# Reordering the seven-product groups of the two down projections in a macaron transformer layer on one Trainium2 core

## The reference

```python
def swiglu(x, w_gate, w_up, w_down):
    return (jax.nn.silu(x @ w_gate) * (x @ w_up)) @ w_down
...
    f = swiglu(rmsnorm(h, g_ffn1_pre[i]), w_ffn1_gate[i], w_ffn1_up[i], w_ffn1_down[i])
    h = h + 0.5 * rmsnorm(f, g_ffn1_post[i])
```

## Time and profile before

| | us |
|---|---|
| runs (3): median, lowest, highest | 1903.43, 1902.51, 1903.64 |
| profiled execution, its own time | 1907.09 |
| its span | 1905.3 |
| TensorE (PE) busy in it | 1868.6 (98%) |
| VectorE (DVE) busy | 1253.8 (66%) |
| ScalarE (ACT) busy | 938.5 (49%) |
| DMA, mean | 195 GB/s |

### The profile page before, as it was taken

How to read it: one execution, slowest core, us unless ns; L and a number is a source line. 1 busy time by engine, 2 the same in 40 slices (tenths; PEclk the granted TensorE clock), 3 DMA queues, 4 the chain that set the end, 5 groups by cost and what they waited for, 6 DMA issues and landing times.

```text
span 1905.3 us, 24370 instructions
## 1 busy us (share of the span) xinstructions
PE 1868.6 (98%) x8562; PEld 1528.3 (80%) x8562; DVE 1253.8 (66%) x1400; ACT 938.5 (49%) x1239; POOL 112.9 (6%) x162
## 2 busy tenths in 40 slices
PE   9999999999999999999999999999999999999998
PEld 7888888888777778888888888888888887777886
DVE  5555554555797778787896755555554579867775
ACT  6444443444455446555565644444443455445563
POOL 1000000000000000012651100000000000000010
PEclk9999999999999999999999999999999999999999
DMA  8666666666555555655556566666666655655654
GB/s 258 206 201 206 194 191 204 217 214 211 198 191 198 159 185 183 201 168 165 157 180 200 165 212 207 203 205 201 200 192 198 221 200 185 209 187 183 213 189 144
DMA packets 214116, 371.55 MB, mean 195 GB/s; under 512 B 16592, under 2 KB 41632, under 8 KB 213664
## 3 DMA queue, kind: packets, MB, share of 16 engines
q1 hardware_dynamic: 213040, 367.20, 61.1%
q10 hardware_dynamic: 1008, 3.46, 0.5%
HBM read 358.01 MB, written 2.10 MB: 189 GB/s over the span
## 4 chain that ended last, share of the span: by engine, by line
PE 81%; DVE 12%; DMA 5%; ACT 1%; SPq 0%; issue 0%; DVEq 0%; POOLq 0%; POOL 0%; ACTq 0%
PE bank L654 26%; PE bank L656 25%; PE bank L655 25%; DVE w_rest L1539 7%; DMA raw<-in_w_ffn_down 5%; DVE branch L1551 1%; DVE branch L1547 1%; DVE branch L1549 1%; DVE branch L1546 1%; ACT w_high L1154 1%; PE bank L993 1%; PE bank L1022 1%; PE bank L1004 1%; PE bank L760 1%; DMA resid<-in_x 0%; PE bank L968 0%
## 5 line engine op out<-in xcount | busy, mean ns | idle before, releaser
L1525 DVE TENSOR_TENSOR w_rest<-raw,w_high 128x1024 fp32r<-128x1024 f32 x486 | 596.8, 1231 | 467.3 <-ACT w_high L1136 464.3
L1136 ACT CAST w_high<-raw 128x1024 fp32r<-128x1024 f32 x486 | 509.6, 1051 | 637.0 <-PE bank L656 493.2
L654 PE MATMUL bank<-w_high,x_high 128*128 128x512 f32 (+1 forms) x1912 | 745.7, 390 | 0.7 <-DVE x_rest L1966 0.2
L656 PE MATMUL bank<-w_high,x_rest 128*128 128x512 f32 (+1 forms) x1912 | 741.0, 388 | 0.0
L655 PE MATMUL bank<-w_rest,x_high 128*128 128x512 f32 (+1 forms) x1912 | 740.6, 387 | 0.0
L654 PEld LDWEIGHTS bank<-w_high,x_high 128*128 128x128 f32 x1912 | 359.1, 188 | 74.6 <-issue 1.6
L656 PEld LDWEIGHTS bank<-w_high,x_rest 128*128 128x128 f32 x1912 | 359.0, 188 | 73.8
L655 PEld LDWEIGHTS bank<-w_rest,x_high 128*128 128x128 f32 x1912 | 359.2, 188 | 71.6
L1539 DVE TENSOR_TENSOR w_rest<-raw,w_high 128x1024 fp32r<-128x1024 f32 x136 | 164.6, 1222 | 78.8 <-ACT w_high L1154 78.4
L1154 ACT CAST w_high<-raw 128x1024 fp32r<-128x1024 f32 x136 | 140.5, 1049 | 114.1 <-DMA raw<-in_w_ffn_down 58.3
L654 PE MATMUL bank<-w_high,h_high 128*128 128x512 f32 x448 | 176.3, 394 | 7.5 <-DVE w_rest L1539 7.5
(11 more groups left out here) (209 smaller groups left out, 1277.0 us busy)
## 6 DMA issues: line engine op xcount, KB each, us to landing
raw<-in_w_ffn_up SPq DMA_DIRECT2D x176, 512.0 KB, 4.6
raw<-in_w_ffn_gate SPq DMA_DIRECT2D x174, 512.0 KB, 4.4
raw<-in_w_ffn_down SPq DMA_DIRECT2D x144, 512.0 KB, 4.8
raw<-in_w_qkv SPq DMA_DIRECT2D x68, 512.0 KB, 4.0
branch<-in_w_ffn_down SPq DMA_DIRECT2D x32, 512.0 KB, 6.7
raw<-in_w_o SPq DMA_DIRECT2D x32, 512.0 KB, 4.2
raw<-in_w_ple_gate SPq DMA_DIRECT2D x32, 512.0 KB, 4.2
branch<-branch SPq DMA_DIRECT2D x320, 32.0 KB, 1.9
```

Of the source, the lines that this page charges most:

```text
L654: nc.tensor.matmul(o[:, 0:width], xh, wh, start=first and c == 0, stop=False, skip_group_check=go_on)
L656: ins = nc.tensor.matmul(o[:, 0:width], xr, wh, start=False, stop=last and c == chunks - 1, skip_group_check=go_on)
L1136: nc.scalar.copy(slot(n, k)[0], raw[:, k]).then_inc(w_high_done, 1)
L1525: nc.vector.tensor_tensor(to_rest, raw[:, k], to_high.bitcast(F32), ALU.subtract).then_inc(w_rest_done, 1)
```

## The change

The table is rewritten: a group's seven products alternate with four plain slots that stand inside it, in the order plain, `b11`, plain, `sum1`, `b22`, plain, `sum3`, `sum2`, `b21`, plain, `sum4`, and groups stand one behind another. Each sum is made right behind the rest of the block that completes it: sum1 behind `b11`, sum3 and sum2 behind `b22`, sum4 behind `b21`. The two in-place buffers change roles from group to group (`FIRST_OF`, `SECOND_OF`), so that the next `b11` goes where `sum3` has been read and the next `b12` where `sum4` has; the first group of j = 0 uses `gain_row` for one of them. The chain loads stand at places of their own in SyncE's queue (`CHAIN_AT`), the first one ahead of the stage; the gain loads follow later. Numbers of matmuls, casts, rests, sums and loads stay as they are.

```diff
     def group(i, inner):
 
-        return ([(kind, None, i) for kind in ("b22", "b21", "b11", "sum1", "sum3", "sum2")] + inner
-                + [("sum4", None, i)])
+        own = [(kind, None, i) for kind in ("b11", "sum1", "b22", "sum3", "sum2", "b21", "sum4")]
+        return inner[0:1] + own[0:1] + inner[1:2] + own[1:3] + inner[2:3] + own[3:6] + inner[3:4] + own[6:]
...
+    PAIR_ORDER = (plains(0, G0, G0 + 5) + group(0, plains(0, G0 + 5, G0 + 9)) + group(1, plains(1, G0, G0 + 4))
+                  + group(2, plains(0, G0 + 9, G0 + 11) + plains(1, G0 + 4, G0 + 6))
+                  + group(3, plains(1, G0 + 6, G0 + 10)) + plains(0, G0 + 11, FS) + plains(1, G0 + 10, FS))
...
-    COMBINE_AT = [0] + [at - 7 for at in GROUP_AT[1:]]
+    def after_op(t):
+
+        return min(u for r, u in enumerate(RING_OPS) if r >= RING and RING_OPS[r - RING] >= t)
+
+    CHAIN_AT = [[RING_OPS[RING]] * 2] + [[after_op(PLACE[end, None, i - 1]) for end in ("sum3", "sum4")] for i in range(1, GROUPS)]
+    FIRST_OF = [["row", 1, 0, 1], [0, 1, 0, 1]]
+    SECOND_OF = [[1, 0, 1, 0], [1, 0, 1, 0]]
+    COMBINE_AT = [0] + [at - 5 for at in GROUP_AT[1:]]
...
+    ODD_STOP = G0 + 9
...
+                def chain_load(j, i, b):
+
+                    if i == 0 and j == 0:
+                        if b:
+                            sp.wait_ge(turned, u_h + BPB)
+                    elif i == 0:
+                        sp.wait_ge(fixed_even, 2 * f + 1)
+                    elif i == 1 and j == 0 and b == 1:
+                        sp.wait_ge(turned, u_h + BPB)
+                    else:
+                        end = "sum4" if b else "sum3"
+                        sp.wait_ge(w_rest_done, n0 + PAIR_OPS * j + PLACE[end, None, i - 1] + 1)
+                    to = chain(j, (SECOND_OF if b else FIRST_OF)[j][i])
+                    sp.dma_start(to, part(2 * i, 2 * j + b)).then_inc(chain_landed[b], 16)
+
+                chain_load(0, 0, 0)
...
+                        for g in range(GROUPS):
+                            for b in range(2):
+                                if t == CHAIN_AT[g][b] and (j, g, b) != (0, 0, 0):
+                                    chain_load(j, g, b)
...
-                            pe.wait_ge(branch_ready, CREDIT - 1 + 2 * NBD * f + 2 * j + 1)
-                            pe.wait_ge(turn_rest, u_h + BPB)
+                            pe.wait_ge(turn_rest, u_h + BPB)
+                        if kind == "b22" and i == 0:
+                            pe.wait_ge(branch_ready, CREDIT - 1 + 2 * NBD * f + 2 * j + 1)
...
-                        if j == 0 and t - 1 in COMBINE_AT:
+                        if j == 0 and t - 2 in COMBINE_AT:
...
+                if kind in ("b11", "b22", "b21"):
+                    turns, other = chain(j, FIRST_OF[j][i]), chain(j, SECOND_OF[j][i])
+                    if kind == "b11":
+                        dve.wait_ge(chain_landed[1], 16 * (groups + i + 1))
+                        nc.vector.tensor_tensor(turns, turns, other, ALU.add).then_inc(sum_ready, 1)
+                    elif kind == "b22":
+                        nc.vector.tensor_tensor(other, other, src, ALU.add).then_inc(sum_ready, 1)
+                        nc.vector.tensor_tensor(turns, turns, src, ALU.add).then_inc(sum_ready, 1)
+                    else:
+                        nc.vector.tensor_tensor(turns, turns, src, ALU.add).then_inc(sum_ready, 1)
...
-                    dve.wait_ge(w_used, n0 + PAIR_OPS * j + PLACE["sum2", None, GROUPS - 1] + 1)
+                    dve.wait_ge(w_used, n0 + PAIR_OPS * j + PLACE["plain", 1, ODD_STOP] + 1)
```

More of the change, by code:

```diff
@@ L479, in down @@
                             sp.dma_start(raw[:, k], src).then_inc(w_landed[k], 16)
-                        if kind == "b22":
-                            for b, end in ((0, "sum4"), (1, "sum3")):
-                                if i:
-                                    sp.wait_ge(w_rest_done, n0 + PAIR_OPS * j + PLACE[end, None, i - 1] + 1)
-                                elif j:
-                                    sp.wait_ge(fixed_even, 2 * f + 1)
-                                else:
-                                    sp.wait_ge(turned, u_h + BPB)
-                                sp.dma_start(chain(j, b), part(2 * i, 2 * j + b)).then_inc(chain_landed[b], 16)
+                        if j == 0 and t == CHAIN_AT[1][1]:
+                            gain_load(0)
+                            gain_load(1)
                         if j and t == GROUP_END[0]:
@@ L1148, in high_down @@
                     act.wait_ge(chain_landed[0], 16 * (groups + i + 1))
-                    src = chain(j, 0)
+                    src = chain(j, FIRST_OF[j][i])
                 else:
                     act.wait_ge(sum_ready, 4 * (groups + i) + SUM_AT[kind])
-                    src = chain(j, 1 if kind == "sum3" else 0)
+                    src = chain(j, (SECOND_OF if kind == "sum3" else FIRST_OF)[j][i])
                 act.wait_ge(w_used, n - RING + 1)
@@ L1532, in rest_down @@
                 groups = GROUPS * (2 * f + j)
-                turns, b12 = chain(j, 0), chain(j, 1)
                 if kind in RING_KINDS:
@@ L1536, in rest_down @@
                 else:
-                    src = b12 if kind == "sum3" else turns
+                    src = chain(j, (SECOND_OF if kind == "sum3" else FIRST_OF)[j][i])
                 dve.wait_ge(w_high_done, n + 1)
@@ L1540, in rest_down @@
                                         ).then_inc(w_rest_done, 1)
-                if kind == "plain" or kind in ("b22", "b21", "sum3", "sum4"):
-                    return
-                b22, b21 = (raw[:, ring_item(j, PLACE[name, None, i])[1]] for name in ("b22", "b21"))
-                if kind == "b11":
-                    dve.wait_ge(chain_landed[1], 16 * (groups + i + 1))
-                    nc.vector.tensor_tensor(turns, turns, b12, ALU.add).then_inc(sum_ready, 1)
-                    nc.vector.tensor_tensor(b12, b12, b22, ALU.add).then_inc(sum_ready, 1)
-                elif kind == "sum1":
-                    nc.vector.tensor_tensor(turns, turns, b22, ALU.add).then_inc(sum_ready, 1)
-                else:
-                    nc.vector.tensor_tensor(turns, turns, b21, ALU.add).then_inc(sum_ready, 1)
+                if kind in ("b11", "b22", "b21"):
[6 more added lines that the diff above has]
+                        nc.vector.tensor_tensor(turns, turns, src, ALU.add).then_inc(sum_ready, 1)
+                    else:
+                        nc.vector.tensor_tensor(turns, turns, src, ALU.add).then_inc(sum_ready, 1)
             def ahead(n, s0, count_, k0=0):
```

33 lines of the change are left out of this document (16 added, 17 removed).

## The result

The changed kernel takes 1884.55 us (median of 4 runs, 1883.42 to 1885.65), the kernel before on the same chip 1902.97 (4 runs, 1902.31 to 1903.64): a ratio of 0.9903, 95% interval 0.9886 to 0.992, 18.4 us less. The forecast was 1875.4 with a range of 1866 to 1889; the result lies in the range, and outside the 1871 to 1882 that had the chance of 0.62. The profiled execution took 1885.05 us, its span 1883.3.

The account below looks back on a forecast made before the run. TensorE, busy 98% of the span, waits in the down stages only for VectorE's rests. Of 39.0 us possible, 5.7 (`combine`) and 4.7 (start) stay, leaving 28.6, taken as 28: median 1903.4 to 1875.4, range 1866 to 1889.

Parts of the forecast that it names:

- What there was to win: Both down stages: 41.1 us too long together, of which up to 39 us can be won.
- Combine, 5.7 us: Later groups of j = 0: third plain slot's rest 0.8 us late plus 0.15 restart, six times; 5.7 us stay.
- In j = 0 `combine` covers it: Groups of j = 0: VectorE's wait for the `b12` load is hidden by `combine`; cost zero.
- The start, 4.7 us: Start of each stage: loads queued behind the one waiting for `turned` make rests late, 2.35 us a stage; 4.7 stay.
- Fifth: just in time: Stage start: fifth slot's load lands at 498.3, its rest ends at 500.7, PE wants it at 500.9.
- j = 1 at zero: Groups of j = 1: VectorE's walk has nothing late, tightest rest 0.8 us to spare; zero stall.
- rival (b): `b12` late everywhere, taking 6.7 us and landing at 2.5: 16.5 us more, 1892; chance 0.15, or part of it.
- (c): Slower: `b12` takes the burst's 9.0 us, lands at 4.8, and the queue's head-of-line wait takes over: 1918; chance 0.04.
- The tail at zero: Stage end: four plain slots (10.9 us) cover even fix, squares and output, some 7 us; cost zero.
- the gain comes from order alone: Down stages: PE's matmuls, casts, rests, sums and bytes stay, so only their reordering brings the gain.
- (a): All stalls go, late j = 0 slots and start absorbed: 1864.4, or 1868 with one term halved; chance 0.14.
- (d): No change: the stall only moves, since VectorE's work is the same; 1903; chance 0.03.

Follow-up runs that it names:

- the second profile: The kernel before, unedited, profiled once more: 1903.39 us, span 1901.6.
- the later chain load: Changed kernel with the chain load that waits for `turned` put two ring loads later in SyncE's queue: 1877.41 us, ratio 0.9866.
- sum1 later: Changed kernel with sum1 made behind P1's rest (the group's second plain slot) instead of in front of it: 1884.4 us, ratio 0.9901.
- the one with slots between: The 1877.41 us kernel (first chain load two ring loads later) with a plain slot put ahead of the second and third group: 1873.67 us.
- the kernel with the shorter tail: The 1873.67 us kernel's two slots between groups, both taken from behind the last group, leaving one even slot there: 1887.17 us.
- the kernel with the seven together: Changed kernel with a group's seven products standing nearly together again, loads, buffers, roles and sum places kept: 1896.77 us, ratio 0.997.
- the kernel with three slots: The 1873.67 us kernel with a third plain slot, ahead of the fourth group, and `fix_odd` one operation earlier: 1874.37 us.

## Why the prediction was right, and where it wasn't

**Right: the sign, what PE waits for, and the place of most of what stays.** PE waits for rests 12 times, where "about 6 + 6, all in j = 0, each under 1.2 us" stood: 11 are in j = 0, and the longest is 1.30. Two of the forecast's own signs of error came: a wait for the fifth slot, and one wait in j = 1. The change won 18.4 us where 28 were forecast, so nearly all terms were too hopeful. The forecast's sum was 39.0 possible less 5.7 less 4.7, taken as 28. Against the profile that it was made from, 22.7 us went from the stages. Its terms:

- *What there was to win* was too large by about 4 us, since it was read from one profiled execution: its first stage was 4.0 us longer than in the second profile. The forecast moved its result by 3.7 us to the median, but took the gain whole, though the excess lay just where the gain was counted. This is the largest single error, 3 to 4 of the 9 us by which the forecast missed.
- *Combine, 5.7 us* ("0.8 us late, and 0.15 for the restart" in each of six groups): measured 7.1 by the gaps, 7.3 by leaving it out. The walk was right in its chain, and in its size too where VectorE doesn't stand for b12: gaps of 1.05 to 1.12 us (three with the later chain load, five with sum1 later) are 0.9 to 1.0 with the restart, and it has 0.95. What it missed is b12. "In j = 0 `combine` covers it" failed in four of six groups, by 0.18 to 0.48 us and 1.3 in all, so in the second group the third slot's rest began at 9.4 on its clock instead of 9.1. Nothing is handed on from group to group, although VectorE's work in such a group, 15 starts of 1.135, one `combine` of 2.86 and one `combine_rest`, is 21.0 us against 20.4 of TensorE: in all six the rest of the first plain slot begins 4.1 us ahead of its product, as the walk has it. A plain slot ahead of the group lets it begin 5.5 us ahead, and that is what removes the gap. The second group's `combine`, which follows that rest by 1.14, and the product, in the changed kernel and in the one with slots between:

```profile
525.38 1.22 DVE L1746 TENSOR_TENSOR branch<-h_high,h_rest 128x1024 f32<-128x1024 f32 x1
...
528.35 0.39 PE L679 MATMUL bank<-w_high,h_high 128*128 128x512 f32 x1
```
```profile
520.15 1.22 DVE L1747 TENSOR_TENSOR branch<-h_high,h_rest 128x1024 f32<-128x1024 f32 x1
...
524.47 0.39 PE L680 MATMUL bank<-w_high,h_high 128*128 128x512 f32 x1
```

- *The start, 4.7 us*: gaps and restarts sum to 3.4 in the first stage and 2.1 in the second, 5.5. "Fifth: just in time" failed in the first stage, where PE stood 1.30 us for it (gap 1.69 at 503.14): its load took 6.5 us from issue, landing at 500.66, and not 498.3, in a row of five that followed 1.3 apart. The cause was named, the queue behind `turned`. The later chain load gives back 7.1 us by the medians: these 5.5, and 0.7 in the combined groups, where VectorE stands less for b12. The rest lies in j = 1 of the first stage and isn't the start's, as said above.
- *j = 1 at zero*: about 1.5 us, beside 0.8 for the transposes at the first stage's end and the 1.0 of the undisturbed half. The only waits, at 671.50 (gap 0.88) and behind, follow a b12 load of 6.5 us, over the "5.6" that the text gave as the limit; those of 5.2 to 5.6 left no gap. This is rival (b), once in six groups. One ring load later, b12 takes 6.1 us, goes out 1.8 later, and the time goes to 1908: the thin cover was thin, and (b) and (c) are one slope. They price 16.5 us more for a landing at 2.5 on the group's clock and 43.5 more at 4.8 (49 less the 5.7 of `combine`); b12 lands at 3.1 to 4.2, 3.8 on average, in j = 1, for which that line gives about 32, and 30.8 were measured. A part of these is the fall of the clock, which the forecast didn't have.
- *The tail at zero*: right here, 0.4 us. With one or two even slots behind the last group instead of three the wait at the first stage's end grows to 1.7 and 1.8 us, except in the kernel whose TensorE is held up by `fix_odd` (0.7).

**Wrong in its reason: "the gain comes from order alone", read as alternation.** The prediction said that a lead of three operations can't absorb a group that stands together. With the new loads and buffers a group that stands together makes no wait in j = 1 at all. There the 16 us come from what the forecast treated as a condition, b12 and b11 asked for early and sums made beside their blocks. Only beside `combine` in j = 0 does the alternation pay; and of j = 0's 16.1 us the change as a whole took 2.7. The forecast left 10.4 us there. That the result still fell inside the range is in part luck: in j = 1 most of the gain came, but for another reason than the one given, and the terms that were too hopeful, all on the same side, summed to 9 us of the 14 that the range allowed upward.

**Rivals.** (a) would have needed both stalls gone; with the first chain load two places later and a slot between groups most of them are, and the time is 1873.7, still above its 1868. (c) and (d) didn't come.

What stays open: which part of the change frees j = 1 (earlier `b11`, earlier `b12`, the first place of `b11`, or the place of the sums), and why the fifth slot's load takes 6.5 us from issue in the first stage of the changed kernel and 5.3 in the second, in the same place of the queue, which makes the gap 1.69 in one and 0.43 in the other.

## What to carry to other kernels

Split a stage's loss by its parts before saying what a change is worth: the half with `combine` and the half without moved by 2.7 and 16 us. Profile the kernel before a second time if the profiled execution lies above the median, and look whether the excess lies where the gain is counted. A wait in an in-order queue is priced by what stands behind it: two loads moved ahead of a waiting one were worth 6 to 7 us, one operation moved ahead of a waiting rest 11.

## What was not expected of the hardware

TensorE's clock falls inside a busy stage, in kernels whose PE is busy 98 or 99% of the span. After TensorE had stood 1.8 to 3.4 us the mean granted clock of the following 4 to 6 us was 0.59 to 0.72, so part of it at 1.2 GHz, with matmuls 0.43 us apart; it cost 1.3 to 1.8 us each time (7 to 9 matmuls at 0.43), beside the wait itself. It didn't follow each wait: behind one of the four gaps of 2.74 in the kernel with the shorter tail, and behind gaps of 2.0 in the kernel with the seven together, the pace stayed 0.23. So a stand of 2.4 us could cost 4, while the many of 1 us in the kernel before cost no more than themselves.

A VectorE operation of 1.22 us took 3.42 beside one of GpSimd that takes 2.40 where it starts first, and 1.74 beside the narrow ones. GpSimd was idle in the stage, and still wasn't free to use in the place that was tried. The same shows on a small scale at the stage's end, where GpSimd's `rstd` took 1.43 us beside VectorE's rests in the kernel with three slots and 0.56 where no rest ran beside it.
